# A two-block transformer kernel: one-hot groups interleaved with 66 early first products, whose activations travel through DRAM

## What is computed

```
# h: 256 tokens x 1024 (normalised x); 8 heads, 16 chosen experts each = 128 (expert, gate) pairs a token
q    = h @ w_query;  sc = q . sub_keys            # two scores lists of 128 a head
top  = best 16 of v1[a] + v2[b]                   # expert number = i1[a] * 128 + i2[b]
gate = softmax(top)
act  = gelu(h @ expert_u[idx])                    # first product
y    = sum over pairs of  gate * act * expert_v[idx]   # second product
out  = rmsnorm(x + y)
```

## Time and profile before

| | |
|---|---|
| median of 3 runs | 1521.38 us |
| the profiled execution: device time | 1520.39 us |
| its span, first to last instruction | 1518.2 us |
| TensorE busy | 1477.2 us (97%) |
| VectorE, ScalarE, GpSimd busy | 908.6, 848.6, 548.8 us |
| mean granted TensorE clock | 0.997 |
| HBM | 236 MB read, 1 MB written |

### The profile page before, as it was taken

The page is one execution under the profiler, slowest core; times in us unless marked ns, Lnnn a source line. Parts: engine busy times, 40 slices in busy tenths (PEclk is TensorE's granted clock), DMA queues, the critical chain, the costliest instruction groups (busy, mean ns, idle before and its releaser), DMA issues.

```text
span 1518.2 us, 24600 instructions
## 1 busy us (share of the span) xinstructions
PE 1477.2 (97%) x8779; PEld 1297.6 (85%) x8779; DVE 908.6 (60%) x2191; ACT 848.6 (56%) x1597; POOL 548.8 (36%) x214
## 2 busy tenths in 40 slices
PE   7999999999999999989999999999999999999998
PEld 6788888788899898889999888888888888888786
DVE  4935259388245531225996976666666666666665
ACT  5556454588356644443557975555555555555554
POOL 6881665700567477455888940000000000000000
PEclk9999999999999999999999999999999999999999
DMA  8750445600334344332551035555555555555564
GB/s 316 280 173 29 166 135 173 220 29 2 111 137 159 122 161 173 139 118 105 181 180 57 1 139 191 187 186 187 191 192 193 193 193 187 187 186 190 179 194 136
DMA packets 43699, 238.36 MB, mean 157 GB/s; under 512 B 4320, under 2 KB 4448, under 8 KB 25440
## 3 DMA queue, kind: packets, MB, share of 16 engines
q1 hardware_dynamic: 43616, 237.27, 45.5%
HBM read 236.21 MB, written 1.05 MB: 156 GB/s over the span
## 4 chain that ended last, share of the span: by engine, by line
PE 64%; ACT 3%; POOL 2%; DVE 2%; issue 1%; ACTq 0%; DVEq 0%
PE bank L1254 23%; PE bank L1277 11%; PE bank L840 6%; PE bank L1280 6%; PE bank L673 4%; PE bank L793 2%; POOL wlo L1321 2%; PE bank L1234 2%; PE bank L676 2%; PE bank L735 1%; PE bank L776 1%; ACT whi L1393 1%; ACT arena L1707 1%; PE bank L969 1%; PE bank L1121 1%
## 5 line engine op out<-in xcount | busy, mean ns | idle before, releaser
L1321 POOL TENSOR_TENSOR wlo<-raw,whi 128x2048 fp32r<-128x2048 f32 (+1 forms) x51 | 195.2, 3839 | 159.2 <-ACT whi L1393 158.9
L1321 POOL TENSOR_TENSOR wlo<-arena,whi 128x2048 fp32r<-128x2048 f32 (+1 forms) x45 | 195.0, 4339 | 152.7 <-ACT whi L1393 152.6
L1254 PE MATMUL bank<-whi,ghi 128*128 128x512 f32 x512 | 200.7, 392 | 1.7 <-DVE glo L2500 1.0
L1254 PE MATMUL bank<-wlo,ghi 128*128 128x512 f32 x512 | 200.4, 391 | 0.0
L1254 PE MATMUL bank<-whi,glo 128*128 128x512 f32 x512 | 199.2, 389 | 0.0
L1277 PE MATMUL bank<-hT,whi 128*128 128x512 f32 x768 | 189.9, 389 | 1.6 <-ACT whi L1739 1.6
L1277 PEld LDWEIGHTS bank<-hT,whi 128*128 128x128 f32 x768 | 144.0, 188 | 31.7 <-ACT whi L1739 1.8
L2487 DVE TENSOR_TENSOR wlo<-raw,whi 128x1024 fp32r<-128x1024 f32 x84 | 102.8, 1225 | 70.6 <-ACT whi L1746 70.6
L1393 ACT ACTIVATE whi<-arena 128x2048 fp32r<-128x2048 f32 x41 | 78.4, 1915 | 95.1 <-PE bank L793 28.7
L1746 ACT ACTIVATE whi<-raw 128x1024 fp32r<-128x1024 f32 x84 | 88.7, 1057 | 76.3 <-PE bank L1254 73.8
L793 PE MATMUL bank<-whi,hT 128*128 128x512 f32 x512 | 125.8, 392 | 0.0
(11 more groups left out here) (333 smaller groups left out, 3047.9 us busy)
## 6 DMA issues: line engine op xcount, KB each, us to landing
raw<-ex_in SPq DMA_DIRECT2D x64, 1024.0 KB, 4.8
raw<-w_in SPq DMA_DIRECT2D x44, 1024.0 KB, 5.2
arena<-w_in SPq DMA_DIRECT2D x44, 1024.0 KB, 5.2
xw<-ex_in SPq DMA_DIRECT2D x32, 1024.0 KB, 4.8
raw<-ex_in SPq DMA_DIRECT2D x54, 512.0 KB, 4.2
xw<-ex_in SPq DMA_DIRECT2D x10, 512.0 KB, 4.3
arena<-frt_in SPq DMA_DIRECT2D x1, 3904.0 KB, 15.6
arena<-tab_in SPq DMA_DIRECT2D x1, 1089.0 KB, 18.6
```

What stands on the lines that cost most here:

```text
L1254: last = mm(bank[2 * t + h][:, :], g[:, j % 2, tok], w[:, b, at], start=False, stop=(final and i == 2), skip_group_check=True)
L1321: last = G.tensor_tensor(wlo[:, u % 2, at], slots[u % RING][:, at], whi[:, u % 2, at], ALU.subtract)
```

## The change

Only the expert layer is edited. NL falls from 98 to 62, so NA rises from 30 to 66: 36 tiles move from the rounds to the early stage and the tail. The groups of W no longer have a stage: group n stands behind the first product of early tile 29 + n, for n = 0 to 31 (`groups_at`). W of all tiles now goes to the arena, so `kept_w` and `weigh_ahead` go away. The early activations are put into three small buffers (`staged`), stored to a DRAM tensor `spill` (128 KB a tile), and in the tail loaded again and weighed by VectorE (`weigh_again`). The rings of raw U and of split U have four slots up to tile 23 and three from tile 24 on, since the fourth slot holds one-hots; the one-hots have two buffers each where they had four. ScalarE weighs one of the eight tokens of a group (it was two), GpSimd seven.

```
-NL = 2 + XBODY * 16
+NL = 2 + XBODY * 10
-ACT_GATES = 2
+ACT_GATES = 1
-SEL1_AT = 28
+SEL1_AT = 27
+G0 = 29
+RAW_OF = [i % 4 if i < G0 - 5 else i % 3 for i in range(NA)] + [0, 1, 2, 0]
+SPLIT_OF = [i % 4 if i < G0 - 5 else i % 3 for i in range(NA)] + [0, 1, 2, 3]
+def groups_at(i):
+    return range(i - G0, i - G0 + 1) if G0 <= i < G1 else range(0)
+        staged = [gact[:, 0], gact[:, 1], xw[:, 3 * T:4 * T]]
+        spill = nc.dram_tensor("spill", (NA, P, T), FP32, kind="Internal").ap()
-        ahead_act = [arena[:, T * (NL + i):T * (NL + i) + T] for i in range(NA)]
+        act_again = [arena[:, 14 * T + T * (m % 32):14 * T + T * (m % 32) + T] for m in range(NA)]
...
@@ SP
+            def store_act(i):
+                sp_.wait_ge(aa_gelu, i + 1)
+                sp_.dma_start(spill[i], staged[i % 3]).then_inc(act_stored[i % 3], 16)
...
-                    sp_.wait_ge(aulo_ready, i - 3)
+                    sp_.wait_ge(aulo_ready, before(RAW_OF, i) + 1)
...
+                sp_.dma_start(aslots[RAW_OF[i]], rows_of_u).then_inc(aex_loaded[RAW_OF[i]], 16)
+                if i >= 6:
+                    store_act(i - 6)
...
             for i in range(NL, N_KEYS):
                 sp_.wait_ge(vlo_ready, i - XRING - 1)
                 sp_.dma_start(xslots[ex_slot(i)][:, D:2 * D], ex_d[i][:, D:2 * D]).then_inc(ex_loaded[ex_slot(i)], 16)
+                m = i - NL
+                if m >= 4:
+                    sp_.wait_ge(g_ready, i - 3)
+                sp_.dma_start(act_again[m], spill[m]).then_inc(act_back[m % 4], 16)
...
@@ TensorE
+            def w_group(n):
+                first, second = first_hot[n % 2], second_hot[n % 2].bitcast(FP32)
+                pe.wait_ge(hotB, n + 1)
+                pe.wait_ge(hotA, n + 1)
+                pe.wait_ge(hotC, n + 1)
+                for h in range(2):
+                    if n == 0:
+                        pe.wait_ge(aa_gelu, G0 - h)
+                    else:
+                        pe.wait_ge(wt_taken, 8 + 2 * (n - 1) + h + 1)
+                    for j in range(4):
+                        last = mm(wbank[h][:, P * j:P * j + P], first[:, 4 * h + j, :], second[:, 4 * h + j, :],
+                                  start=True, stop=True)
+                    last.then_inc(wt_done, 1)
...
+                early_product(i, aa_done)
...
+                for n in groups_at(i):
+                    w_group(n)
...
-            w_groups(pe, w_group)
@@ GpSimd
-            def weigh_ahead(n, at):
-                G.tensor_tensor(at, kept_w[n % 3], at, ALU.mult).then_inc(wm_taken, 1)
...
+            for i in range(NA + 4):
                 pool.wait_ge(auhi_ready, i + 1)
+                G.tensor_tensor(alo[SPLIT_OF[i]], aslots[RAW_OF[i]], ahi[SPLIT_OF[i]], ALU.subtract).then_inc(aulo_ready, 1)
+                for n in groups_at(i - 1):
+                    w_gates(n)
...
@@ ScalarE
             for i in range(NA):
                 act.wait_ge(aa_done, i + 1)
-                A(ahead_act[i], bank[6 + i % 2][:, 0:T], ACT.Gelu_apprx_tanh).then_inc(aa_gelu, 1)
-                ahead_hi(i + 4)
+                if i >= 3:
+                    act.wait_ge(act_stored[i % 3], 16 * (i // 3))
+                A(staged[i % 3], early_bank(i)[:, 0:T], ACT.Gelu_apprx_tanh).then_inc(aa_gelu, 1)
+                for n in groups_at(i):
+                    w_out(n)
+                for j in range(i + 1, NA + 3):
+                    if before(SPLIT_OF, j) == i:
+                        ahead_hi(j)
+                for n in groups_at(i + 1):
+                    w_gates(n)
...
@@ VectorE
+            def weigh_again(i):
+                if i < N_KEYS:
+                    m = i - NL
+                    w = Wg[:, T * i:T * i + T]
+                    dve.wait_ge(act_back[m % 4], 16 * (m // 4 + 1))
+                    V.tensor_tensor(w, act_again[m], w, ALU.mult).then_inc(g_ready, 1)
```

More of the change, by code:

```diff
@@ L31, with before @@
 XBODY = 6
-NL = 2 + XBODY * 16
+NL = 2 + XBODY * 10
 NA = N_KEYS - NL
 E_AT = (12, 23)
-ACT_GATES = 2
+ACT_GATES = 1
 SEL0_AT = 19
-SEL1_AT = 28
+SEL1_AT = 27
+G0 = 29
+GROUPS_W = T // 8
+G1 = G0 + GROUPS_W
+HEAD = [(NA + 2 * tile + part, tile, part) for tile in range(2) for part in range(2)]
+RAW_OF = [i % 4 if i < G0 - 5 else i % 3 for i in range(NA)] + [0, 1, 2, 0]
+SPLIT_OF = [i % 4 if i < G0 - 5 else i % 3 for i in range(NA)] + [0, 1, 2, 3]
+LAST_OF_FOUR = G0 - 6
+def before(ring, i):
+    earlier = [j for j in range(i) if ring[j] == ring[i]]
+    return earlier[-1] if earlier else None
+def groups_at(i):
+    return range(i - G0, i - G0 + 1) if G0 <= i < G1 else range(0)
 SCALE = HD ** -0.5
@@ L236, in build @@
         auhi_ready, aulo_ready, aa_done, aa_gelu = (sem(n) for n in ("auhi_ready", "aulo_ready", "aa_done", "aa_gelu"))
-        wm_taken = sem("wm_taken")
+        act_stored = [sem(f"act_stored{i}") for i in range(3)]
+        act_back = [sem(f"act_back{i}") for i in range(4)]
         b_taken, sum_ready = sem("b_taken"), sem("sum_ready")
@@ L392, in build @@
         iota_ps = bank[4][:, 0:P]
-        wbank = bank[5:8]
-        kept_w = [xw[:, 3 * T + 8 * NA * i:3 * T + 8 * NA * i + 8 * NA].rearrange("p (n t) -> p n t", t=8) for i in range(3)]
+        wbank = bank[6:8]
         QP = R[:, 0:4096].rearrange("p (b t) -> p b t", b=16)
@@ L519, in build, with early_bank @@
         ysq = arena[:, 3 * D:3 * D + CW]
[L521 to L525, removed]
+        head_bank = [bank[5 + (NA + n - G1) % 3] for n in range(2)]
+        head_first = [q for q in HEAD if q[2] == 0]
+        def early_bank(i):
+            return bank[6 + i % 2] if i < G0 else bank[5] if i <= G1 else bank[5 + (i - G1) % 3]
         def ex_slot(i):
@@ L622, in _ @@
             sp_.wait_ge(out_stored, 64)
[L624 to L632, removed]
         def expert_loop(engine, iteration):
@@ L1205, in _ @@
                     pe.wait_ge(wt_taken, 7 + i)
-                else:
[L1207 to L1211, removed]
+                elif i < G0:
+                    pe.wait_ge(aa_gelu, i - 1)
+                elif i == G0:
+                    pe.wait_ge(tr_taken, tr_all("sel0"))
+                elif i <= G1:
+                    pe.wait_ge(aa_gelu, i)
+                elif i <= G1 + 2:
+                    pe.wait_ge(wt_taken, 8 + T // 4 + i - G1 - 2)
+                else:
+                    pe.wait_ge(aa_gelu, i - 2)
+                early_product(i, aa_done)
                 if i == SEL0_AT:
@@ L1687, in ahead_hi, with w_out, w_gates @@
                 else:
-                    act.wait_ge(aa_done, i - 3)
-                A(ahi[i % 4], aslots[i % 4], ACT.Copy).then_inc(auhi_ready, 1)
+                    act.wait_ge(aa_done, before(SPLIT_OF, i) + 1)
+                A(ahi[SPLIT_OF[i]], aslots[RAW_OF[i]], ACT.Copy).then_inc(auhi_ready, 1)
+            W4 = arena[:, :].rearrange("p (n g t) -> p g t n", g=T // 4, t=4)
+            def w_out(n):
+                for h in range(2):
+                    act.wait_ge(wt_done, 2 * n + h + 1)
+                    A(W4[:, 2 * n + h], wbank[h][:, :].rearrange("p (t n) -> p t n", t=4), ACT.Copy).then_inc(wt_taken, 1)
+            def w_gates(n):
+                hot = first_hot[n % 2]
+                act.wait_ge(hot_ready, n + 1)
+                for j in range(8 - ACT_GATES, 8):
+                    last = A(hot[:, j, :], hot[:, j, :], ACT.Copy, scale=gates[:, n, j:j + 1])
+                last.then_inc(hotC, 1)
             for i in range(4):
```

141 lines of the change are left out of this document (53 added, 88 removed).

## The result

| | before | changed |
|---|---|---|
| median of 4 runs each, us | 1520.77 (1519.65 to 1522.84) | 1510.88 (1510.81 to 1512.84) |
| ratio, 95% interval | | 0.9937 [0.9919, 0.9954] |
| span of the profiled execution, us | 1518.2 | 1509.8 |
| granted clock | 0.997 | 0.995 |

The account below looks back on a forecast made before the run. TensorE, busy 97% of the span, was taken to bound the kernel, with GpSimd bounding the new group stage. Terms: -72.0 + 39.0 + 3.1 + 2.5 + 0.4 = -27.0 us, giving 1494.4 us; range 1484 to 1509.

Parts of the forecast that it names:

- the first reading: W stage: matmul starts 0.118 us apart, a group of eight 0.95 us, TensorE's own work 30 us, some 42 to gain.
- 32 x (4.10 - 2.88) = +39.0: Early stage: a group behind each of 32 tiles lengthens the period from 2.88 to 4.10 us, +39.0 us.
- gap: Ahead of the rounds: TensorE waits for the heads' activations; 2.3 us with GpSimd idle, 3.6 busy, 2.5 taken.
- tail start: Ahead of the first tail tile: one more VectorE multiplication, +0.4 us.
- GpSimd as the bound: Group stage: GpSimd's remainder and gates need 4.07 to 4.12 us, more than TensorE's 3.83; 4.10 a period taken.
- TensorE bounds: Rival, group stage: it runs at TensorE's 3.83 us a period, 8.6 us less, 1485.8 us; chance 0.17.
- 1510 to 1518, chance 0.05: Rival: smaller gain from a store wait, a U load wait with three slots, or longer unrolled code; chance 0.05.
- The chain: Rival, group stage: four-engine chain, some 7.6 us against two periods of 8.2; if longer, 1504 to 1510 us; chance 0.2.
- near 0.1 us for a moved tile: 36 tiles moved from rounds to early stage and tail: 36 x (2.88 + 2.72 - 5.515) = +3.1 us.
- the DMA share of the tail: Tail: the reload adds a quarter by bytes, share from 0.62 to 0.78, no wait.
- 2.2 us for the reload: Tail loads: 136 KB in rows of about 1 KB landed in 2.2 us, half of what a V half takes.
- Nothing for it: Early stage stores: 256 KB landed in 2.7 us, issued over 5 us ahead of the GELU needing them; no cost.

Follow-up runs that it names:

- doubled products: Each group matmul issued twice into the same place: in the changed kernel 1566.29 us, in the kernel before 1562.39 us.
- The halved run of the kernel before: The kernel before with four of the eight matmuls of each group: 1520.73 us, ratio 1.0001.
- the best version: Changed kernel with fp32r group matmuls, two gates on ScalarE, and ScalarE's rounding of the next U ahead of its copies of W: 1481.37 us.
- the run with half of the products: The changed kernel with four of the eight one-hot matmuls of each group: 1494.91 us, ratio 0.9827.

## Why the prediction was wrong

**The step that failed** is the first reading, "0.118 us apart, so a group of eight needs 0.95 us", and "TensorE's own work in it is 32 x 0.95 = 30 us" after it. The spacing was nearly right (0.118 us, with the wait between two groups in it; 0.111 where nothing waits), and the count was wrong. An fp32 matmul of this kernel leaves two rows, each with its weight load; `x16` in the earlier trace rows is one group and not two. The names in those rows say so too: first the one-hot in `whi`, then the one in `wlo`, one of them for each group, and the order of the program has x8 for each where the trace has x16. A group is 1.78 us. Two runs show that price directly (doubled products: +1.78 us a group after the change, +1.33 before it, where the other 0.46 fell into the slack of the stage), and the row counts say it without a run: 512 rows of L1234 over 32 groups are 16. Even the earlier trace rows had it, with TensorE busy for 68 of 72 us. The halved run of the kernel before shows what some 29 us of work look like there (259 rows of 0.111 us): 48.17 us busy, more than the work but far from 68. The text set that number aside in favour of the spacing, and so explained the contradiction away.

**What followed from it.** Of the forecast's terms, "32 x (4.10 - 2.88) = +39.0" was in truth 32 x 1.775 = +56.8. That is +17.8 us, and it covers the miss almost alone: -27.0 + 17.8 = -9.2, with +1.65 for the clock -7.6, and the small terms (gap -0.3, tail start -0.4) give about -8.3, the measured difference of the spans.

**GpSimd as the bound** was right in size (2.37 + 1.69 = 4.06 us; gates forecast at 1.66 to 1.72) and irrelevant, since TensorE needs 4.66. The rival "TensorE bounds" had the right engine but the price of 0.95 in it: with 1.78 it would have read 2.88 + 1.78 = 4.66 and 1512. The forecast and this rival shared one misread number, so the one was no check on the other. The measured time falls into "1510 to 1518, chance 0.05", but none of the causes named there (a store, a U load, longer code) made TensorE wait.

**The chain** was looked for in the wrong place. The one through four engines has two periods of time, and no run shows it as the bound. The chain that did bind when TensorE was made light runs through ScalarE in one period (copies, rounding, next gates); taking the gates' 0.68 us and their start out of it by reordering brought the period from 4.46 to 4.07 us.

**What held.** The rounds at 5.515 and a tail tile at 2.72 us; near 0.1 us for a moved tile; the DMA share of the tail, 0.78 forecast and 0.77 measured; no wait on a U load with three slots. The transfers themselves were forecast too short: 2.2 us for the reload, where 4.1 was measured, hidden because the tail leaves room.

**What held by luck, or not quite.** Of the stores the prediction said "Nothing for it". ScalarE waited for one twice, 1.79 us where the groups begin (813.65) and 2.20 us close to the end of the early stage, and TensorE waited at neither. The second wait put a GELU 0.65 us late (at 974.30, after 970.77 and a tile of 2.88), and with it the rounding and GpSimd's last two remainders; that they would have ended at about 979.8, before the gap's multiplications, is an estimate. In the gap, 2.5 us was forecast and 2.2 measured, but two errors offset each other in it: with GpSimd idle the forecast was 2.3 us, and 1.73 was measured. The two multiplications took 0.95 us while GpSimd's last remainder (978.08 to 980.45) ran beside them, and 0.49 in the best version, where it did not. In the run with half of the products the remainder ran until 964.91, 1.06 us into them, and they took 1.41. That agrees with the Trainium skill (SBUF — State Buffer, "SBUF: two separate sides"), by which a VectorE instruction with two SBUF inputs and a GpSimd instruction that reads SBUF exclude each other. The line rate for pieces of 512 B and more in the Trainium skill (DMA: Bandwidth & Descriptors, "Specifications") also fits the tail's share. It is no statement on the time from issue to landing, and there the estimate from the earlier trace rows missed.

**What was not foreseen** is the clock behind the gap, +1.65 us. Two things stay open: what decides whether it falls there, and the second level of the run with twelve more early tiles.

## What to carry to other kernels

Before work is moved from a stage under cover into one where an engine has none, divide that engine's rows in the stage by the number of steps of the program, rather than read one step off a spacing; where the window says 95% busy and your reckoning says 42%, the reckoning is what to doubt, even though busy times overstate the work. Covered work costs its full price once it stands in a stage that the same engine bounds: 1.78 us a group here, where in the old stage halving the products changed nothing. Where two cases of a forecast rest on the same number, they are no bounds for each other; and a loop of one period through an engine that serves several others is found by writing down, for each wait, what stands in that engine's program between the release it takes and the release it gives.

## What the runs showed of the hardware that was not expected

- A 128x128 matmul of the program in fp32 takes two rows of 0.111 us, in fp32r one: 1.78 against 0.89 us for eight.
- After an idle time of 2.18 us TensorE began at full clock and fell to the lower level 1.5 us later, for 3.4 us, at a cost of 1.65 us. Of six profiled gaps of 2.18 to 2.86 us, four had the lower clock behind them, after the longest from the first matmul on (5.8 us at 0.50), and two (2.50 and 2.64 us) had none; of three gaps of 1.72 to 1.73 us none had it. The length of the idle time alone does not decide it. In the two runs where matmuls filled the gap the clock was 1.00, which is too few to call the filling the cause.
- 128 KB to DRAM landed in 3.7 us and 128 KB back in 4.1, nearly what 512 KB took (3.9): here the landing did not follow the bytes. With a second reload in the tail, at a DMA share of 0.91, a reload took 4.8 us.
- Two VectorE multiplications with both inputs in SBUF took 0.49 us alone, and 0.95 or 1.41 us when a GpSimd instruction was at work on SBUF for the first 0.60 or 1.06 us of them.
- The program with twelve more early tiles took 1510.8 us in two executions and 1515.2 in three, and the profile shows no cause for it.
